# A bidirectional SSD and attention trunk: VectorE's states ahead of the x convolution in the scan's first group, and TensorE's sums of da one step of K later

## What is computed

```python
proj = h @ w_in                                   # z, x, B, C and dt
xbc = silu(conv5(xbc) + conv_b)                   # depthwise, 5 taps, centred
xs, bm, cm = split(xbc)                           # 32 heads of 64; 8 groups of B, C with 128 states
dt = softplus(dt + dt_bias); a = -exp(a_log)      # for each direction
# one direction; chunks of 128 positions, A = dt * a
a_cs   = cumsum(A)                                # inside a chunk
y_diag = einsum(C, B, exp(a_cs_l - a_cs_s), X)    # inside the chunk
states = einsum(B, exp(a_cs_end - a_cs), X)       # what a chunk hands on
new    = carry * exp(a_cs_end) + states           # scan over the 4 chunks
y_off  = einsum(C, carry, exp(a_cs))              # from the chunks before
y = y_diag + y_off                                # both directions, + xs * d_skip
y = rmsnorm(y * silu(z)) @ w_out
```

## Time and profile before

| | |
|---|---|
| time, median of 3 runs | 758.59 us (758.39 to 758.66) |
| the profiled execution's own time | 758.61 us |
| its span, first to last instruction | 756.8 us |
| mean granted TensorE clock | 0.999 |
| TensorE busy | 746.4 us (99%), 3876 instructions |
| VectorE, ScalarE, GpSimd busy | 471.3, 409.7 and 453.8 us (62, 54 and 60%) |

### The profile page before, as it was taken

The page is one execution under the profiler, slowest core; times in us unless marked ns, Lnnn a source line. Parts: engine busy times, 40 slices in busy tenths (PEclk is TensorE's granted clock), DMA queues, the critical chain, the costliest instruction groups (busy, mean ns, idle before and its releaser), DMA issues.

```text
span 756.8 us, 11707 instructions
## 1 busy us (share of the span) xinstructions
PE 746.4 (99%) x3876; PEld 614.8 (81%) x3876; DVE 471.3 (62%) x889; ACT 409.7 (54%) x823; POOL 453.8 (60%) x263
## 2 busy tenths in 40 slices
PE   7999999999999999999999999999999999999997
PEld 6888888888888888888888888878877888878776
DVE  4777868585867768586851111365756576666756
ACT  7665664739375564839432244355545556556631
POOL 7474875848495776756794335754654546554461
PEclk9999999999999999999999999999999999999999
DMA  8366464644626355543723324413213132130003
GB/s 252 90 225 173 161 145 161 168 168 111 204 72 167 141 142 181 149 168 83 251 86 113 90 83 111 133 56 106 83 57 108 55 99 84 61 107 28 29 1 112
DMA packets 100197, 91.11 MB, mean 120 GB/s; under 512 B 5456, under 2 KB 87728, under 8 KB 97080
## 3 DMA queue, kind: packets, MB, share of 16 engines
q1 hardware_dynamic: 95936, 67.25, 30.4%
q10 hardware_dynamic: 4088, 23.24, 10.0%
q0 software_dynamic: 128, 0.05, 0.0%
HBM read 88.13 MB, written 2.39 MB: 120 GB/s over the span
## 4 chain that ended last, share of the span: by engine, by line
PE 93%; issue 2%; DVE 2%; ACT 1%; POOL 1%; DVEq 0%; ACTq 0%; POOLq 0%
PE bank L1607 76%; PE bank L1782 3%; PE bank L1754 2%; PE bank L1767 2%; PE bank L1936 2%; PE bank L1966 1%; PE bank L1726 1%; PE bank L1739 1%; PE bank L1628 1%; PE bank L1617 1%; PE bank L1835 0%; PE bank L1952 0%; ACT rows L816 0%; PE bank L1736 0%; ACT bank L816 0%
## 5 line engine op out<-in xcount | busy, mean ns | idle before, releaser
L526 POOL TENSOR_TENSOR w_lo<-w_raw,w_hi 128x1024 fp32r<-128x1024 f32 x104 | 255.1, 2457 | 197.3 <-ACT w_hi L692 193.3
L1607 PE MATMUL bank<-hn_hi,w_hi 128*128 128x512 f32 x376 | 150.2, 399 | 0.0
L1607 PE MATMUL bank<-hn_hi,w_lo 128*128 128x512 f32 x376 | 146.9, 391 | 0.0
L1607 PE MATMUL bank<-hn_lo,w_hi 128*128 128x512 f32 x376 | 146.4, 389 | 0.0
L692 ACT CAST w_hi<-w_raw 128x1024 fp32r<-128x1024 f32 x104 | 108.4, 1045 | 68.6 <-PE bank L1607 63.7
L1607 PE MATMUL bank<-w_hi,hn_hi 128*128 128x512 f32 x316 | 127.4, 403 | 0.4 <-ACT qkvz L993 0.4
L1607 PE MATMUL bank<-w_hi,hn_lo 128*128 128x512 f32 x316 | 123.5, 391 | 0.0
L1607 PE MATMUL bank<-w_lo,hn_hi 128*128 128x512 f32 x316 | 123.3, 390 | 0.0
L1149 DVE SCALAR_TENSOR_TENSOR c_acc<-bank,par,c_acc 128x510 f32<-128x510 f32 (+1 forms) x128 | 95.9, 749 | 27.5 <-ACT c_acc L742 18.7
L927 ACT ACTIVATE ex<-sbias,stat 128x512 f32<-128x512 f32 x64 | 45.8, 720 | 76.3 <-DVE stat L1387 76.2
L1607 PEld LDWEIGHTS bank<-hn_hi,w_lo 128*128 128x128 f32 x376 | 70.6, 188 | 15.1
(11 more groups left out here) (254 smaller groups left out, 1290.9 us busy)
## 6 DMA issues: line engine op xcount, KB each, us to landing
w_raw<-in_ssd_w_in SPq DMA_DIRECT2D x48, 512.0 KB, 4.3
w_raw<-in_attn_w_in SPq DMA_DIRECT2D x64, 256.0 KB, 3.1
rows<-acs_rows ACTq DMA_DIRECT2D x14, 1024.0 KB, 5.7
edec<-exp_rows ACTq DMA_DIRECT2D x16, 512.0 KB, 6.4
w_raw<-in_ssd_w_out SPq DMA_DIRECT2D x16, 512.0 KB, 3.6
w_raw<-in_attn_w_out SPq DMA_DIRECT2D x16, 256.0 KB, 3.0
wbias<-bias_rows SPq DMA_DIRECT2D x8, 448.0 KB, 4.2
rows<-in_x SPq DMA_DIRECT2D x4, 512.0 KB, 5.2
```

Source lines behind the costliest of these rows:

```text
L526: nc.gpsimd.tensor_tensor(w_lo[:, s, :], w_raw[:, s, :], f32(w_hi[:, s, :]), ALU.subtract)\
L1607: ins = T.matmul(dst, a[i], b[j], start=first and n == 0, stop=last and n == 2)
```

## The change

Two edits, both round the first group of the scan. On VectorE, in slot 2 of `ssd_iteration(0, 0)`, `scan_ops` stands ahead of `conv`; in all other groups it stays behind it. On TensorE, `acs_sums` is put in after step 5 of K instead of step 4. Nothing else changes, on no other engine.

```diff
                     if scan and slot == 1:
                         pair_sums(m * 2 + half, range(HPG) if first else (3,))
                         pair_weights(m * 2 + half)
+                    if scan and slot == 2 and first:
+                        scan_ops(0, slot, half)
                     if slot in slots and slot >= 2:
                         conv(m, half, slot)
-                    if scan and slot == 2:
+                    if scan and slot == 2 and not first:
                         scan_ops(m * 2 + half, slot, half)
...
             ins.then_inc(unit_done, 1)
-            project(-1, 1, 3, 4, acs_sums)
+            project(-1, 1, 3, 5, acs_sums)
             project(-1, 1, 4, 4, acs_columns)
```

## The result

The changed kernel takes 762.83 us (median of 6 runs, 762.64 to 763.23), the kernel before 758.66 us (758.39 to 758.71) beside it: a ratio of 1.0054, 95% interval 1.0044 to 1.0065. It is 4.2 us slower; 762.8 us was forecast.

A forecast was written before the change was run, and what follows sets the result against it. The prediction took TensorE, holding 93% of the chain that ended last, to bound the kernel. It summed 758.61 + 2.75 (later start of the products with the states) + 1.4 (slow clock) = 762.8 us, range 760.9 to 763.9.

The forecast's parts named there:

- The sums of da: TensorE, sums one K step later: their 0.34 us wait goes but lengthens the wait before the products with the states; worth 0.
- The states: VectorE, first group: last state ready at 67.7 instead of 70.77 us, but ScalarE's copy of the middle state also releases TensorE.
- The wait: TensorE before the products with the states (L1782): ScalarE's copy, queued behind the later convolution's tanh, delays their start by 2.75 us.
- The clock: TensorE after 3.43 us idle: clock falls 2.16 us into the gap, slow stretch of 3.99 us, costing 1.4 us.
- A longer slow stretch: Rival, TensorE behind the gap: whole 2.0 us loss falls on work, plus 0.3 us of late buffers; 763.7 us, chance 0.13.
- the rival with the clock held: Rival, TensorE before the products with the states: only the 2.75 us delay counts, no slow clock; 761.4 us, chance 0.29.
- The sum: Whole kernel: 758.61 + 2.75 + 1.4 = 762.8 us, 0.55% slower.
- Nothing given back: TensorE's three later waits (0.4, 0.3, 0.3 us) move along; late instructions behind L1782 cost 0, up to 0.3 us more.
- not slower: Rival, ScalarE's copy L783 ends before 70.20 us: both TensorE waits vanish, 0.68 us gained, 757.9 us; chance 0.06.

## Why the prediction was right

*The sums of da.* Right that no wait is left there and that most of the gain turns up in the next wait (0.34 to 0.56 us with this edit alone). Wrong in one step: the chain to the states was said not to hang on TensorE's pace here, and ScalarE's tanh of z did, by some 0.2 us.

*The states.* Right that they come 2.75 us earlier (70.77 to 68.02) and that this helps nobody, since a second releaser had ended only 0.03 us ahead of the one that the profile named. The runs with the copy moved show that this releaser is the cause: ahead of the tanh, all of the loss is gone; right behind it, 3.2 us are (762.83 to 759.63), the 1.6 us of the wait and, since the clock of that kernel held in its profile, the 1.6 us of the slow stretch.

*The wait.* Forecast +2.75 us and 761.4 us without the clock; measured 761.40 and 761.43 with VectorE's edit alone in the two runs whose clock held, and with both edits and work inside the wait 761.38 and 761.14, which is 2.66 and 2.43 us above the kernel before beside them. That the second is lower fits the 0.2 us of the edit on TensorE, which the forecast had at nothing. The chain of tanh, cast, evacuation and copy kept its steps of before to 0.01 us (73.20 - 71.06 = 2.14 against 2.15).

*The clock.* The fall was right, and its price came out near (1.4 forecast, 1.63 measured), but two parts of that term were off and cancelled. The forecast put the fall into the gap, 2.16 us after the work, as at the end of the trace of before; it came 1.2 us after the work had resumed. And it took 3.99 us for the slow stretch, from the start of the trace; it was 3.4 us. Since all of it lay on work, half of 3.4 us was lost. That none of the stretch lay in the gap is what the rival "A longer slow stretch" said, and not the forecast; its price, 763.7 us, had the stretch too long.

Both rows behind the term can be read better. At the start, 16 of the 20 transposes stand 0.21 us apart and the rest 0.11; the timeline up to 7.62 us has the 16:

```profile
4.36 3.56 PE L1617 MATMUL bank<-ident 128*128 128x128 f32 x16 [4.36 <-POOL ident L500]
```

The last of these 16 starts at 7.61 us, so half speed lasted 3.3 us there and not 3.99. And the clock of 1.00 in the earlier trace rows does not disagree: the trace's first record of the clock is at 7.65 us, and a window without a record reads 1.00. In all ten profiles the pace changes at that first record; in the changed kernel's it is at 10.3 us, which is the long slow opening seen above. So the start of the trace was no evidence for the rival with the clock held. At the end, 2.16 us is one value among ten: the fall came 2.2 to 3.6 us after the last matmul in six of the profiles, and in the other four not within the 3.7 us that were left of the span. The kernel with the copy ahead, from its last matmul to its end:

```profile
753.31:757.05 3.74, 0.00 (x0) 0.00 (x0) 1.08 (x2) 0.00 (x0) 0.00 (x0) 1.00 0.78 292
```

With that spread the moment of the fall could not be forecast from one trace.

The sentence of the Trainium skill's page "TensorE: Matmul & The Clock Gate" (section "HAM oscillation — how this bites in real kernels") on slow bursts behind idle gaps is borne out, by their mean clock, by the six runs of the changed kernel and by three of five with VectorE's edit alone, though in the trace the burst does not start slow but turns slow after 1.2 us; in the other two the clock held over the same gap.

*The sum.* 762.8 us forecast and 762.83 measured agree better than the terms do: the wait was put 0.1 to 0.3 us too long and the slow stretch 0.2 us too cheap. That these cancel is luck.

*Nothing given back.* Right for the changed kernel: the three later waits are unchanged. That the late instructions behind the wait cost nothing held only because TensorE was as late as they were. With the wait gone, about 1 us of them came to light, and the rival "not slower", 757.9 us, would have needed the rows moved too; its price was right (758.06 us with both), its condition incomplete.

## What to carry to other kernels

Where an instruction waits for several semaphores, look at every releaser's end and not only at the one that the profile names, and ask of each what stands ahead of it in its own engine's order: moving work up on one engine makes what it passed late, and that holds everything queued behind on the engine that reads it. A wait on the bounding engine can cost more than its length, where the clock falls behind it: after waits of 3.1 to 3.3 us it did in nine of eleven runs here; if such a wait can't be removed, work of no use inside it can be worth more than idleness. And before a wait of that engine is removed, find the next one and what it hangs on, for that is where the gain goes.

## What was not expected of the hardware

The lower clock came late: TensorE idled 3.28 us at 1.00, worked 1.2 us at 1.00, and then lost half its clock for 3.4 us while it was busy. A slow stretch in a profile can thus belong to an idle one that lies ahead of work at full speed. And the price of a fixed wait was not fixed: 761.4 or about 763 us, in runs of one kernel. The opening varies in the same way: TensorE's first transposes ran at half speed up to 7.5 us of the span in one profile and up to 10.4 in another, and VectorE's first `hn_lo` came at 12.52 and 13.11 us.
